# Weighing two heads on the two column halves of TensorE, with the values held and the probabilities streamed

## The reference

```python
# A) 8 latent-attention heads ("M"), chunk-causal mask, keys of 64 + 32, values of 64
s = (einsum("bqhd,bkhd->bhqk", qn, k_nope) + einsum("bqhd,bkd->bhqk", qr, kr_all)) * mla_scale
w = softmax(where(mask, s, -1e30))
mla = einsum("bhqk,bkhd->bqhd", w, v_mla)
# B) 4 retention heads, chunkwise recurrent, group norm, swish gate
# C) 4 stick-breaking heads ("S"), strictly causal
zz = einsum("bqhd,bkhd->bhqk", qs, sk_all) * sb_scale
log_beta = log_sigmoid(zz)
log_1mb = where(mask, log_beta - zz, 0)
after = cumsum(log_1mb, reverse=True) - log_1mb
sb = einsum("bhqk,bkhd->bqhd", where(mask, exp(log_beta + after), 0), sv_all)
mix = concatenate([mla, ret, sb], axis=-1) @ w_o
```

## Time and profile before

| | |
|---|---|
| median of 3 runs | 1728.07 us (1727.09 to 1733.08) |
| the profiled execution | 1736.33 us, its span 1734.6 us |
| TensorE busy | 1656.1 us, 95% of the span |
| VectorE, ScalarE, GpSimd busy | 1068.8, 608.7, 169.0 us |
| chain that ended last | PE 86%, DVE 5%, ACT 5% |
| mean granted clock of TensorE | 0.970 of full speed |

### The profile page before, as it was taken

How to read it: one execution, slowest core, us unless ns; L and a number is a source line. 1 busy time by engine, 2 the same in 40 slices (tenths; PEclk the granted TensorE clock), 3 DMA queues, 4 the chain that set the end, 5 groups by cost and what they waited for, 6 DMA issues and landing times.

```text
span 1734.6 us, 27429 instructions
## 1 busy us (share of the span) xinstructions
PE 1656.1 (95%) x9986; PEld 1496.5 (86%) x9986; DVE 1068.8 (62%) x2325; ACT 608.7 (35%) x1198; POOL 169.0 (10%) x226
## 2 busy tenths in 40 slices
PE   6899999889999999999998999999999999999996
PEld 3599999546766777778997999999999999999996
DVE  3776654457676766665327666665666666665657
ACT  4620010236566667575225222122222222121213
POOL 0011111313222221110210000000000000000000
PEclk9899999989898999996999999999999999999998
DMA  9555545411111110043210111111111111111003
GB/s 326 195 157 164 176 146 184 157 37 42 60 48 48 48 48 5 13 142 141 76 33 25 61 37 49 36 54 43 38 47 36 60 36 48 36 41 56 12 1 116
DMA packets 114221, 133.61 MB, mean 77 GB/s; under 512 B 14954, under 2 KB 91545, under 8 KB 112793
## 3 DMA queue, kind: packets, MB, share of 16 engines
q1 hardware_dynamic: 110809, 121.76, 22.0%
q0 software_dynamic: 3328, 10.73, 1.7%
HBM read 107.47 MB, written 27.23 MB: 78 GB/s over the span
## 4 chain that ended last, share of the span: by engine, by line
PE 86%; DVE 5%; ACT 5%; issue 3%; DMA 1%; SPq 0%; ACTq 0%; DVEq 0%; POOLq 0%
PE psum L2135 34%; PE psum L2199 15%; PE psum L1901 11%; PE psum L2104 6%; PE psum L2084 3%; PE psum L2055 3%; PE psum L2059 2%; PE psum L1987 2%; PE psum L1929 1%; PE psum L1934 1%; PE psum L1805 1%; PE psum L1967 1%; DVE h_lo L1430 1%; PE psum L1827 1%; ACT pT L1170 1%
## 5 line engine op out<-in xcount | busy, mean ns | idle before, releaser
L2135 PE MATMUL psum<-act_hi,wt_parts 128*128 128x362 f32 (+1 forms) x2496 | 615.9, 328 | 9.5 <-DVE act_lo L1430 5.4
L1741 DVE SCALAR_TENSOR_TENSOR residual<-psum,mod,residual 128x364 f32<-128x364 f32 (+2 forms) x704 | 299.8, 495 | 257.4 <-PE psum L2199 257.4
L2135 PEld LDWEIGHTS psum<-act_hi,wt_parts 128*128 128x128 f32 x2496 | 443.2, 189 | 12.4 <-issue 7.0
L2135 PE MATMUL psum<-act_lo,wt_parts 128*128 128x362 f32 (+1 forms) x1248 | 409.5, 328 | 0.0
L2199 PE MATMUL psum<-u_hi,wt_parts 128*128 128x362 f32 (+1 forms) x1056 | 263.1, 330 | 3.0 <-issue 3.0
L2135 PEld LDWEIGHTS psum<-act_lo,wt_parts 128*128 128x128 f32 x1248 | 235.9, 189 | 0.0
L2199 PEld LDWEIGHTS psum<-u_hi,wt_parts 128*128 128x128 f32 x1056 | 187.9, 189 | 3.3 <-issue 3.3
L2199 PE MATMUL psum<-u_lo,wt_parts 128*128 128x364 f32 (+1 forms) x528 | 174.6, 331 | 0.0
L1901 PE MATMUL psum<-w_hi,h_hi 128*128 128x308 f32 x512 | 158.2, 309 | 2.7 <-DVE h_lo L1430 2.1
L1901 PE MATMUL psum<-w_lo,h_hi 128*128 128x308 f32 x512 | 156.7, 306 | 0.0
L1901 PE MATMUL psum<-w_hi,h_lo 128*128 128x308 f32 x512 | 156.1, 305 | 0.0
(11 more groups left out here) (236 smaller groups left out, 2237.4 us busy)
## 6 DMA issues: line engine op xcount, KB each, us to landing
wt_raw<-in_w_up SPq DMA_DIRECT2D x44, 512.0 KB, 3.9
ada_raw<-in_w_ada SPq DMA_DIRECT2D x32, 512.0 KB, 3.9
wt_raw<-in_w_down SPq DMA_DIRECT2D x22, 512.0 KB, 4.4
w_raw<-in_w_in SPq DMA_DIRECT2D x16, 616.0 KB, 5.6
z_scratch<-z_out POOLq DMA_DIRECT2D x64, 154.0 KB, 3.0
z_in<-z_scratch SPq DMA_DIRECT2D x8, 1232.0 KB, 5.3
ada_first<-in_w_ada SPq DMA_DIRECT2D x16, 512.0 KB, 11.8
xT_scratch<-xT SPq DMA_DIRECT2D x1, 4352.0 KB, 19.1
```

Of the source, the lines that this page charges most:

```text
L1741: last = dve.scalar_tensor_tensor(out=res[:, d, a:b], in0=bank[4 + q % 4][:, a - CHUNKS[c][0]:b - CHUNKS[c][0]], scalar=mod[:, 40 + d, whi ...
L2135: last = pe.matmul(out[:, :b - a], ww[:, slot, P * k:P * k + P], aa[:, k, a:b], start=(k == 0 and m == 0), stop=(k == KT - 1 and m == 2))
```

## The change

- The weights of an M head are scaled before the transpose instead of the output after the weighing: VectorE writes a diagonal matrix with the reciprocal row sums (`spread_scale`: L1689, L1690), one step after the unit's own, and TensorE multiplies the block by it (L2157) instead of transposing it against the identity. TensorE waits for it (`s_nd`). S heads are transposed as before.
- Weighing is done for two heads of a kind at once (`PAIRS`), after the second has been copied. The values are held, 128 keys by 64 columns, and `pT` is streamed, 128 columns. The first head of a pair writes PSUM partitions 0 to 63, the second 64 to 127, so each uses a half of the array's columns, and the result is already transposed (L2180). `pT` has eight pieces instead of four.
- `head_output` is replaced by `pair_output` (L1707), one copy of 128x128 to `mixT` or `mix_raw`. Only the retention's 256 columns still go through `mixtok` and an X transpose, two blocks instead of eight, at `MIX_STEP` 6.
- Each pair's rows are stored by a transfer of their own, seven per tile instead of one.
- To make room, some small buffers of the rotation, the gate and the norms are shared or moved (`rope_a`, `junk`, `oc`), with one more wait of ScalarE for itself in `prepare`.

```diff
-MIX_STEP = 17
+MIX_STEP = 6
...
+def plan_pairs():
+
+    out = {}
+    for n in range(NTILE):
+        for kind, heads in (("M", H_MLA), ("S", H_SB)):
+            for h in range(0, heads, 2):
+                units = tuple(12 * n + KINDS.index((kind, x)) for x in (h, h + 1))
+                out[units[1] + T_LAG[kind] + 1] = (n, kind, h // 2, units)
+    return [(step, *out[step]) for step in sorted(out)]
...
+            def store_pair(v):
...
+                sp.wait_ge(s_o, v + 1)
+                if n < NTILE - 1:
+                    store_mix(n, mix_block(kind, p), 1)
...
+                free = pair_before(n, kind, UNITS[i][2] // 2)
+                if free is not None:
+                    act.wait_ge(s_pv, free + 1)
...
+            def spread_scale(i):
+
+                r, u = rows_of(UNITS[i][0]), count_units("M", i)
+                dve.wait_ge(s_p, u + 1)
+                if u >= 2:
+                    before = [x for x in range(i) if UNITS[x][1] == "M"][-2]
+                    dve.wait_ge(s_tr, last_piece("M", before) + 1)
+                ch.link(dve.reciprocal(rowsum[:r, u % 4, 1:2], rowsum[:r, u % 4, 0:1]))
+                dve.tensor_scalar(spread[:r, u % 2, :r], ident[:r, :r], rowsum[:r, u % 4, 1:2], None, ALU.mult)\
+                    .then_inc(s_nd, 1)
...
+            def pair_output(v):
+
+                _, n, kind, p, _ = PAIRS[v]
+                r, b = rows_of(n), mix_block(kind, p)
+                dve.wait_ge(s_pv, v + 1)
...
+                dve.tensor_copy(out, bank[pv_bank(v)][:, P * (v % 4):P * (v % 4) + r]).then_inc(s_o, 1)
...
-                for x in PIECES.get(step - 1, []):
-                    if x[0] != "X" and x[2] == 0:
-                        head_output(x[1])
+                if step in PAIR_AT:
+                    pair_output(PAIR_AT[step])
                 if 0 <= step - 2 < len(UNITS) and UNITS[step - 2][1] == "S":
                     stick_sums(step - 2)
+                if 0 <= step - 1 < len(UNITS) and UNITS[step - 1][1] == "M":
+                    spread_scale(step - 1)
...
+                        if kind == "M":
+                            last = pe.matmul(to, of, spread[:r, u % 2, :r], start=True, stop=True)
+                        else:
+                            last = pe.transpose(to, of, ident[:r, :r])
...
-                    last = pe.matmul(bank[pv_bank(v)][:r, 64 * (v % 8):64 * (v % 8) + 64], pT[:size, W_NO[x] % 4, k % 4, :r],
-                                     vals, start=(k == 0), stop=(k == len(blocks) - 1))
...
+                    for a, i in enumerate(units):
+                        h = UNITS[i][2]
+                        vals = v_mla[:size, tile_, 64 * h:64 * h + 64] if kind == "M" else \
+                            sv[:size, tile_, 64 * h:64 * h + 64]
+                        last = pe.matmul(bank[pv_bank(v)][64 * a:64 * a + 64, P * (v % 4):P * (v % 4) + r], vals,
+                                         pT[:size, piece_slot(kind, i, k // 4), k % 4, :r],
+                                         start=(k == 0), stop=(k == len(blocks) - 1))
```

More of the change, by code:

```diff
@@ L194, in count_units, with pair_before, mix_block @@
     return sum(k == kind for _, k, _ in UNITS[:i])
+def plan_pairs():
[6 more added lines that the diff above has]
+    return [(step, *out[step]) for step in sorted(out)]
+PAIRS = plan_pairs()
+PAIR_NO = {x[1:4]: v for v, x in enumerate(PAIRS)}
+PAIR_AT = {x[0]: v for v, x in enumerate(PAIRS)}
+LAST_PAIR_STEP = PAIRS[-1][0]
+def pair_before(n, kind, p):
+    v = max((v for v, x in enumerate(PAIRS) if x[2] == kind and (x[1], x[3]) < (n, p)), default=None)
+    return v
+def mix_block(kind, p):
+    return p if kind == "M" else 6 + p
 def plan_pieces():
     steps = {}
-    for step in range(12 * (NTILE - 1) + MIX_STEP + 1):
+    for step in range(LAST_PAIR_STEP + 1):
         out = []
@@ L208, in plan_pieces @@
         if rest == 0 and 0 <= n < NTILE:
-            out += [("X", n, 0), ("X", n, 1)]
+            out += [("X", n, 0)]
         steps[step] = out
@@ L217 @@
 PIECE_NO = {x: q for q, x in enumerate(ORDER)}
-W_NO = {x: w for w, x in enumerate(x for x in ORDER if x[0] != "X")}
-N_PIECES = len(W_NO)
-PV_ORDER = [x[1] for x in ORDER if x[0] != "X" and x[2] == 0]
-PV_NO = {i: v for v, i in enumerate(PV_ORDER)}
-PV_STEP = {x[1]: step + 1 for step in range(STEPS) for x in PIECES[step] if x[0] != "X" and x[2] == 0}
 PV_LAST_LOW, PV_FIRST_TAIL = 12 * 5 - 2, 12 * 8 + 1
 def pv_bank(v):
-    step = PV_STEP[PV_ORDER[v]]
-    if v % 2 and 12 <= step <= PV_LAST_LOW:
+    step, _, kind, _, _ = PAIRS[v]
+    if kind == "S" and 12 <= step <= PV_LAST_LOW:
         return 1
-    if v % 2 and step >= PV_FIRST_TAIL:
+    if kind == "S" and step >= PV_FIRST_TAIL:
         return 7
@@ L395, in build @@
         zero = s3("zero", [1])
-        gate = s3("gate", [256])
-        oc = s3("oc", [H_RET, DH])
-        oc2 = s3("oc2", [H_RET, DH])
+        spread = s3("spread", [2, P])
         stat = s3("stat", [4, H_RET])
@@ L712, in store_state, with store_mix, store_tile @@
                     sp.dma_start(heads, part).then_inc(s_out, 16)
-            def store_mix(n):
+            def store_mix(n, b, count):
                 r, t = rows_of(n), SEQ[n]
-                pieces_done(sp, ("X", n, 1))
-                sp.dma_start(mixT_dram[:, :, P * t:P * t + r], mixT[:, :, :r]).then_inc(s_mst, 16)
+                sp.dma_start(mixT_dram[:, b:b + count, P * t:P * t + r], mixT[:, b:b + count, :r])\
+                    .then_inc(block_stored(b), 16)
+            def store_pair(v):
[3 more added lines that the diff above has]
+                    store_mix(n, mix_block(kind, p), 1)
+            def store_tile(n):
+                for step in range(12 * n, 12 * n + 12):
+                    if step in PAIR_AT:
+                        store_pair(PAIR_AT[step])
+                    if step == 12 * n + MIX_STEP and n < NTILE - 1:
+                        pieces_done(sp, ("X", n, 0))
+                        store_mix(n, 4, 2)
             store_latent(0)
@@ L1128, in softmax_exp @@
                 if j >= 4:
-                    act.wait_ge(s_o, 1 + PV_NO[[x for x in range(i) if UNITS[x][1] == "M"][-4]])
+                    act.wait_ge(s_nd, j - 3)
                 act.activation(prob[:r, j % 3, :w], score_bank(i, w)[:r], ACT.Exp, bias=maxes[:r, j % 2, 1:2],
@@ L2070, in transposes @@
                     r = rows_of(i)
-                    if j == 0:
-                        pe.wait_ge(s_ret, i + 1)
-                        pe.wait_ge(s_o, 12 * (i + 1))
-                    for k in range(4):
-                        last = pe.transpose(out[:, P * k:P * k + r],
-                                            mixtok[:r, i % 2, P * (4 * j + k):P * (4 * j + k) + P], ident[:r, :r])
+                    pe.wait_ge(s_ret, i + 1)
+                    for k in range(2):
+                        last = pe.transpose(out[:, P * k:P * k + r], mixtok[:r, i % 2, P * k:P * k + P], ident[:r, :r])
                 else:
@@ L2083, in transposes, with weigh @@
                     for k, (col, size, _) in enumerate(key_blocks(n)[4 * j:4 * j + 4]):
-                        last = pe.transpose(out[:size, P * k:P * k + r], src[:, col - first:col - first + size],
-                                            ident[:r, :r])
+                        to, of = out[:size, P * k:P * k + r], src[:, col - first:col - first + size]
+                        if kind == "M":
+                            last = pe.matmul(to, of, spread[:r, u % 2, :r], start=True, stop=True)
+                        else:
+                            last = pe.transpose(to, of, ident[:r, :r])
                 last.then_inc(s_tr, 1)
-            def weigh(i):
-                n, kind, h = UNITS[i]
-                r, v = rows_of(n), PV_NO[i]
+            def weigh(v):
+                _, n, kind, p, units = PAIRS[v]
+                r = rows_of(n)
                 if pv_user_before(v, pv_bank(v)) is not None:
@@ L2112, in _ @@
                     scores(step)
-                for x in PIECES.get(step - 1, []):
-                    if x[0] != "X" and x[2] == 0:
-                        weigh(x[1])
+                if step in PAIR_AT:
+                    weigh(PAIR_AT[step])
                 for x in PIECES.get(step, []):
```

118 lines of the change are left out of this document (65 added, 53 removed).

## The result

The changed kernel is slower: 1775.25 us (median of 4 runs, 1768.51 to 1778.17) against 1727.78 us for the kernel before on the same chip, ratio 1.026, 95% interval 1.0235 to 1.0285. It lies outside the range that I gave, 1702 to 1768, and on the other side of my forecast of 1719.

What follows compares the result with a forecast made beforehand. TensorE was taken to bound the large tiles. TensorE's terms -5.3, the wait +3 and the last steps -7 gave -9.3 us, from 1728.07 to 1718.8, forecast 1719; range for 8 in 10: 1702 to 1768.

Steps and rivals of the forecast that it cites:

- the price and the wait of `spread`: VectorE's product behind the stick operations: 0.281 us each, TensorE waiting 1.7 us in tile 8, about +3 (0 to +8).
- The wait for `spread` eats it: Rival: TensorE waits for `spread` at every S step of the five larger tiles, +8 to +10, 1728; chance 0.05.
- Item 1: M transposes on TensorE become two-row products with `spread`: +31.0 us for 272, +3 for the sample tile's 40.
- Items 2 and 4: TensorE: paired weighing at 0.058 us a row, -39.2 (-42.3 to 0); shape changes of 0.19 and 0.09, +7.
- rival on the halves: Weighing: halves one after the other, up to 1765, chance 0.3; or loads in line, 0.081 a row, 1737, chance 0.2.
- my first rival: Weighing: the halves run one after the other, two heads save nothing, +37, up to 1765; chance 0.3.
- Tile 7: Sign: forecast wrong if query tile 7 lasts longer than 60.90 us; it should take about 59.
- The last steps: Chain after the last scores to the first output projection: -7 us, between -1.5 and -12; `spread` ready 6.4 after weighing starts.
- Item 3: X transposes on TensorE fall from 8 to 2 per tile: 46 fewer, -5.1 us, and -2 of idle time.

Runs made afterwards that it cites:

- the run with single rows: Changed kernel without reciprocal and spread product, M blocks transposed against the plain identity, outputs not divided by row sums: 1712.13 us, ratio 0.9885.
- the one with doubled rows: Changed kernel without spread product on VectorE, M blocks multiplied by the identity in ordinary two-row matmuls: 1723.05 us, ratio 0.9971.
- the heads in turn: Early-place kernel, but head 0 of a pair weighs all its blocks before head 1, each in its own half: 1756.16 us, ratio 1.0148.
- early-place kernel: Changed kernel with `spread_scale` called right behind its step's row maximum or logits, ahead of pair copy and stick operations: 1732.76 us, ratio 1.002.
- the short subtraction: Changed kernel, `spread_scale` at its late place, GpSimd's subtraction behind each scan on an eighth of its columns: 1730.43 us, ratio 1.001.

## Why the prediction was wrong

**The step that failed is the price and the wait of `spread`** in "The change on the other engines". I put 0.281 us on the product, from L1335, and from that "at two places of twelve steps ... 1.7 us of wait in tile 8, about +3", with 0 to +8 as its bounds. The wait was 49.6 us. L1335 is the same operation, but its nine rows stand in the first 46 us, where GpSimd's subtraction doesn't run. Right behind the scan it does, and the earlier trace rows has that scan at its end without asking whom it releases. So the sum took for granted that VectorE's product can overlap with GpSimd's work, and that is what failed. The order showed the product behind the scan; the trace of before had the operation that starts there (L885), and even a line that was held by GpSimd, which I didn't read (duration min/median/max):

```profile
L1550 DVE TENSOR_TENSOR qtok<-q_a,q_b x18: 282/292/1303, 349.2 to 702.2; 128x128 f32<-128x128 f32 x16, 64x128 f32<-64x128 f32 x2
```

A maximum of 1303 ns on a line with a median of 292 and one width is no matter of width: at 427.6 it stands beside the rotation L842, and at 389.0 (0.63 us) and 702.2 (0.50) beside the subtraction, 0.15 us past its end each time. The Trainium skill states the rule (SBUF — State Buffer, Who interferes with whom): VectorE and GpSimd share a pair of ports as an exclusive lock; a `tensor_scalar` from SBUF to SBUF can take it, a VectorE operation with two SBUF inputs contends with GpSimd's reads, and the second to issue blocks until the first is done. These traces agree: beside GpSimd's long operations L1690 ends 0.05 to 0.09 us and L1606 0.15 us behind GpSimd's end, and those with a source in PSUM are not held. By the rows above, the term should have been 36 products that last as long as the subtractions beside them (L885, 52.0 us in sum before) in place of 36 x 0.29, some 41 us of VectorE's time, and the call's place a rival with a chance of its own. "The wait for `spread` eats it" had 0.05 and +8 to +10 us, with the right place and a fifth of the price, since it too held the product to be short. What the waits did to TensorE's clock, 19 us of the 51 between two profiles, no term of mine had.

**Item 1 was too large for the large tiles and too small for the sample tile.** The products take 0.112 us a row, x576, as forecast. But +31.0 and +3 on TensorE's stream became 11 us of the kernel. In tiles 6 to 8, 152 products times 0.114 are 17.3 us, and 12 were measured; in tiles 1 to 5 nothing (120 products, 13.7 us at that price), where the run with single rows is at clock 0.90 and the one with doubled rows at 0.97; in the last steps -4.6, at 0.86 against 1.00; and in the sample tile 8.7 in place of 3. "In the large tiles a microsecond taken out of TensorE's stream is a microsecond of the kernel" is the sentence that doesn't hold: of 60.90 us it was idle for 1.20, but with less work it waits for ScalarE's copies (23.0 us in the run with single rows) and its clock falls. Ten rows in the sample tile take 1.33 us at the upper clock and 2.36 at the lower, five transposes took 0.51; its stretch had clock 0.89 before, and 0.70 after.

**Items 2 and 4 were right:** by the lengths of the groups above, a row takes 0.0545 where I took 0.058 (0.054 was my lower bound), and the ends of a group 0.15 where I took 0.19 and 0.09; together 0.060. Neither rival on the halves came true. That it rests on alternation was shown by the heads in turn. They lose 23 us of a stream that is longer by 37 (the distances between starts within weighing add up to 88.7 us, four waits left out, against 51.4), again two thirds. Serial halves, as in my first rival, would have taken the early-place kernel to about 1769, its further copies included.

**Tile 7** lasts 65.80 us, so by my own mark the forecast is wrong. Without the hold it lasts 59.2, in the early place, with the short subtraction and without a product alike, and I had said about 59.

**The last steps** were right in size and partly in the working. From the weighing to the first projection matmul they took 27.2 us, and now 21.3: -5.9, with -7 forecast and -1.5 to -12 as bounds. The product for unit 106 is ready 8.3 us behind the weighing's start, not 6.4, because the longest product of all (2.41 us) lies on this chain:

```profile
833.20 1.97 PE L2180 MATMUL psum<-pT,v_mla 128*64 128x128 f32 x32 [0.23 <-ACT pT L1226]
...
839.03 2.34 POOL L936 TENSOR_TENSOR esb<-zsb,esb 128x1024 f32<-128x1024 f32 x1 [15.20 <-DVE esb L1680]
839.05 2.41 DVE L1690 TENSOR_SCALAR spread<-ident_sb,rowsum 128x128 f32<-128x128 f32 x1
...
841.60 5.68 PE L2157 MATMUL psum<-spread,prob 128*128 128x128 f32 x32 [5.41 <-DVE spread L1690]
...
854.53 0.57 PE L2210 MATMUL psum<-act_hi,wt_parts 128*128 128x364 f32 x2 [1.67 <-DVE act_lo L1739]
```

In the early place the same stretch takes 17.4 us, -9.9, so the close match with -7 is in part luck: the hold on this chain took back what the clock gave (0.85 in the changed kernel's last stretch, 0.55 before).

**The sum without the hold.** The changed kernel with no product of VectorE's takes 1723.05 us, 5.4 under the kernel before; my terms without the wait gave -12.3. The sample tile alone, 58.2 us there against 47.7 before, makes 10.5 - 3 = 7.5 us of difference. So TensorE's part was out by about 7 us. The whole error is larger: +47.5 was measured and -9.3 forecast, 57 us apart. The hold is 42 to 45 of them (early place, short subtraction); the rest are those 7 and the product's cost without most of the hold, 9.7 where I had put +3. In the early place, with everything computed, the change comes out at ratio 1.002, no gain: the sum was too low even without the neighbour.

Item 3 (X transposes; six of its 46 are the sample's, 64x64 and not of full size) was not tried by itself. What of the hold's cost falls on which later wait of VectorE's queue stays open, beyond the split of 30 and 22.

## What to carry to other kernels

Before an operation on VectorE from SBUF to SBUF is priced by a row elsewhere, look in the timeline at what GpSimd does at the new place: here the same product took 0.29 us in one place and up to 2.41 in another, a few lines apart in the code, and the kernel 42 us more. Read min, median and max of a line, not its mean; where the maximum was far above the median at one width here, it was a neighbour's doing. Two heads on the two halves of the array paid here because their matmuls alternate. And price an idle gap of TensorE above its length, and a microsecond off its stream below it: here the same matmuls took 19 us longer in the kernel that waited more, and a microsecond off the stream was worth a third to two thirds of one (11 us for some 34, 23 for 37).

## What the runs showed of the hardware

- VectorE's SBUF-to-SBUF `tensor_scalar` of 128 columns and `tensor_tensor` with both inputs in SBUF stand still while a GpSimd operation on SBUF that started before them runs: 36 of 36 products lasted as long as the subtraction beside them, and when its mean went from 1.40 to 0.34 us theirs went from 1.46 to 0.42. It works the other way too: in the early kernel with the probabilities scaled in place the product starts 0.08 us ahead of the rotation L893 at 584, keeps its 0.55 us, and the rotation takes 1.64 in place of 1.27.
- An fp32 matmul with 64 held and 128 streamed columns took 0.061 us a row when the two halves alternate, 0.100 when each half has its rows in a run, and 0.115 with all in one half (24 rows to a group). Under these lie 0.109 a row within a half, two halves at once where both have rows at hand, and 0.15 a group; where a run of one half met a run of the other, four rows of each stood side by side.
- VectorE's product in place, clear of GpSimd, took 0.286 us on 128 columns, 0.42 on 384 and 0.754 on 1024; the median of its line, 0.511, mixes the widths.
